# Hybrid decoder step: block choice, sample softmax and attention in one stage of two interleaved threads

## The chip, the cores and the metric

One core of one Trainium2 chip. The metric is device time in microseconds (us) of one execution of the whole kernel; less is better. TensorE is also called PE, VectorE DVE, ScalarE ACT, GpSimd POOL; SP is the queue that mostly issues DMAs.

## The reference

One inference step of a two-layer decoder, all in float32, on a prompt of 512 tokens and on 8 sample sequences of 4 new tokens each, whose past of 4096 tokens lies in a paged cache (32 pages of 128 tokens a sequence, found by a page table). A layer applies one input projection, four parallel mixers (convolution, pooling, sparse attention, gated DeltaNet), an output projection and a feed-forward. The change concerns the sparse attention, with 4 heads, 2 key/value heads (two heads share one) of 64 channels. Each query is answered by three branches, whose outputs are weighted by gates and added:

```python
kc = compress_blocks(k_cmp, ...)            # branch 0: one key per 16 tokens
p_cmp = masked_softmax(q . kc + bias, d_cmp >= 0)
imp = p_cmp summed over the 64-token blocks
top = the 16 best blocks (first, current and previous forced)
o_sel = softmax over the tokens of those blocks . v_sel    # branch 1
o_win = softmax over the last 512 tokens . v_win           # branch 2
o = g0 * o_cmp + g1 * o_sel + g2 * o_win
```

The scores get a relative position bias. For the prompt, 512 tokens are 8 blocks, so all are selected and branch 1 is causal attention.

## The kernel before

Activations are kept transposed (channels on partitions): S.xT is the residual stream, S.yT collects the mixers' outputs, S.HT the projection. A loop runs over the two layers. Inside it, each `stage` (L151) is a block in which every engine has its own instruction stream, tied to the others by semaphores; a stage ends with a barrier of all engines (L161). A layer's stages in order: projection, convolution and pooling, natural_keys, sample_scores (L884), then the part of this change, then gated_delta (L1511, first stage "gnorm") and mix_and_feed_forward.

sample_scores loads keys and values to be compressed and keys to be scored, compresses keys and values of the cache, and leaves the raw scores of the samples: rows are the 128 (sequence, head, token) triples, columns are tokens, in p_sel (128 x 4128) and p_win (128 x 544). At L989 and L1033 it uses weights of 32 columns whose results go to four groups of 32 PSUM partitions.

The part of this change consists of three stages in before:

- **"top"** (sample_softmax, L1156). Gates, softmax of branch 0 over 255 compressed keys, sums per block, and two rounds of "eight largest" give block_bias (L1226), which is a large negative number for blocks that are not selected. PE also computes the compressed values (L1184). Nearly all of it is a chain on DVE with short trips to PE and ACT.
- **"soft"** (L1230). DVE adds block_bias to p_sel (L1254) and takes the maximum (L1264), ACT computes the exponential (L1281). PE then multiplies each 128-column piece with a diagonal of gate over sum (L1244), which transposes and scales it at once; ten groups of tiles are copied to st_sel, st_win and pt_new.
- **"att"** (attention_outputs, L1292). The prompt's work is cut into N = 48 units (query tile i, head h, branch br). A unit: scores on PE (L1383, contraction of 64 rows), bias and maximum on DVE (L1482 to L1484), exponential on ACT (L1451), transpose on PE (L1393), copy on ACT (L1461), values on PE (L1407), and the product with the gate over the sum on DVE, added to o (L1499, L1502); the widths are 31 or 128 (i + 1) columns. PE's stream runs three units at once, one step apart. Between them stands sample_third (L1353): for sequence b and half h of its pages, a third of the 16 matmuls of L1373, whose weights are 16 columns of st_sel and whose moving data is one page of cached values, 128 x 128. All 40 matmuls of a sequence go into one 16-row accumulation. A float32 matmul is carried out as two instructions, a transpose as one.

The cached values come as DMAs of one page each, 128 rows of 512 bytes (L1330), 256 pages per layer. Two buffers of 16 pages (vsel) hold one half of a sequence each. SP issues 12 of the 16 pages of a half and ACT, between its own work, 4. The page number must be in a register of the issuing queue, which page_numbers (L554) loads four at a time (L557). SP also loads the window values (L1340), 256 KB, and at the start the bias strip (L1346):

```python
for h in range(2):
    if not first:
        sp.wait_ge(s.part, b * 2 + (h - 1))
    ...
    for first_page in range(0, by_sp, 4):
        fetch(sp, mybir.EngineType.SP, b, h, first_page, pages[h])
```

s.part counts halves that PE has summed. An engine's instructions are issued in the order written; a wait holds up all that stands behind it on that engine.

## Time and profile before

| | us |
|---|---|
| median of 3 runs | 3021.0 (3011.27 to 3021.8) |
| the profiled execution, its own time | 3015.42 |
| its span, first to last instruction | 3013.5 |
| PE busy | 2706.2 |
| DVE busy | 916.5 |
| ACT busy | 578.1 |
| POOL busy | 237.3 |
| "top", "soft" and "att" in the first layer | 528.65 to 737.3 |
| the same in the second layer | 2014.0 to 2218.8 |

Times of the rows count from the span's start. In a list by line, a row gives line, engine, operation, output <- inputs, shape, count, then busy time in us, mean ns of one, and the idle time of the engine before them with what ended it. PEld is the weight load, which runs beside PE. A row of a stretch gives its ends and length, then busy time and, in brackets, instructions of PE, PEld, DVE, ACT and POOL, as far as they are asked for, then the granted clock of TensorE (1.00 is 2.4 GHz, 0.50 is 1.2 GHz), the DMA engines' busy share and GB/s. SPq and ACTq are the queues' DMA instructions.

### The profile page before, as it was taken

What the parts mean: (1) busy time and instruction counts of PE and PEld (TensorE: products, weight loads), DVE (VectorE), ACT (ScalarE), POOL (GpSimd) and SP (SyncE); (2) the same over time, 40 slices, a digit from 0 to 9 for tenths busy, and PEclk for the clock granted to TensorE, in tenths of its full rate; (3) what the DMA queues carried; (4) which work ended last, traced back from release to release, by engine and by line L of the source; (5) the groups of instructions that cost most, each with busy time, mean ns of one, the idle gap of its engine ahead of it and who ended that gap; (6) DMA issues with size and microseconds to landing.
All of it is one profiled execution on the core that took longest, in us unless ns stands there. A gap on an engine that the chain in (4) does not pass through costs nothing. (4 is left out here: it accounts for less than half of the span.)

```text
span 3013.5 us, 45104 instructions
## 1 busy us (share of the span) xinstructions
PE 2706.2 (90%) x17236; PEld 2206.2 (73%) x17236; DVE 916.5 (30%) x2207; ACT 578.1 (19%) x1224; POOL 237.3 (8%) x328
## 2 busy tenths in 40 slices
PE   6996999698698999999969879978968989999997
PEld 4885887566585888888758668865757768888885
DVE  2742333443543210000118223343544322110002
ACT  0013332223310200000110223322242103000002
POOL 0500000000130100000005000000002101000000
PEclk8997999789695999999979989997987779999998
DMA  5205775242001134022042257733410021331220
GB/s 193 78 28 157 223 222 157 82 118 79 2 22 50 48 106 126 28 66 74 0 139 70 49 188 220 219 98 111 126 43 1 22 92 42 111 113 28 56 56 30
DMA packets 343596, 276.93 MB, mean 92 GB/s; under 512 B 61473, under 2 KB 339106, under 8 KB 343002
## 3 DMA queue, kind: packets, MB, share of 16 engines
q1 hardware_dynamic: 316840, 253.71, 28.6%
q10 hardware_dynamic: 26546, 20.35, 2.2%
q8 instruction: 140, 2.29, 0.3%
q14 instruction: 70, 0.57, 0.1%
HBM read 264.14 MB, written 18.17 MB: 94 GB/s over the span
## 5 line engine op out<-in xcount | busy, mean ns | idle before, releaser
L2169 PE MATMUL psum<-xT,up_ring 128*128 128x272 f32 x2048 | 470.3, 392 | 0.0
L2169 PEld LDWEIGHTS psum<-xT,up_ring 128*128 128x128 f32 x2048 | 389.1, 190 | 80.3
L2188 PE MATMUL psum<-ff,HT 128*128 128x272 f32 x1536 | 353.6, 392 | 0.0
L2188 PEld LDWEIGHTS psum<-ff,HT 128*128 128x128 f32 x1536 | 291.8, 190 | 60.2
L368 PE MATMUL psum<-xT,w_ring 128*128 128x272 f32 x1408 | 326.9, 395 | 7.8 <-PEq L161 4.0
L368 PEld LDWEIGHTS psum<-xT,w_ring 128*128 128x128 f32 x1408 | 269.3, 192 | 65.2 <-DMA w_ring<-in_w_in 4.7
L979 PE MATMUL psum<-cst,cache 128*128 128x128 f32 x1600 | 208.9, 286 | 17.8 <-DMA cache<-in_cache_nsa_kv 11.6
L979 PEld LDWEIGHTS psum<-cst,cache 128*128 128x128 f32 x1600 | 179.0, 145 | 40.4 <-DMA cache<-in_cache_nsa_kv 13.0
L2032 DVE SCALAR_TENSOR_TENSOR xT<-xT,psum 128x544 f32<-128x544 f32 (+1 forms) x42 | 24.2, 584 | 527.9 <-PE psum L2188 441.6
L1009 PEld LDWEIGHTS psum<-chunks,W 64*128 64x128 f32 x2304 | 132.8, 189 | 16.8 <-ACT st_sel L1089 11.7
L1373 PE MATMUL psum<-vsel,st_sel 128*16 128x128 f32 x1024 | 136.4, 286 | 9.2 <-DMA vsel<-in_cache_nsa_kv 9.2
L1009 PE MATMUL psum<-chunks,W 64*128 64x128 f32 (+1 forms) x2304 | 139.5, 277 | 0.0
L2234 DVE TENSOR_SCALAR ff<-psum 128x544 f32<-128x544 f32 x32 | 23.2, 724 | 378.7 <-PE psum L2169 378.7
L1373 PEld LDWEIGHTS psum<-vsel,st_sel 128*16 128x16 f32 x1024 | 97.2, 101 | 47.1 <-issue 17.6
L1009 PEld LDWEIGHTS psum<-st_sel,W 64*128 64x128 f32 x2048 | 116.8, 188 | 16.1 <-ACT chunks L1089 11.7
L2146 PE MATMUL psum<-yT,HT 128*128 128x272 f32 x512 | 121.8, 400 | 5.2 <-PEq L161 5.2
L2286 ACT ACTIVATE ln_sq<-xT 128x272 f32<-128x272 f32 x64 | 22.4, 426 | 531.1 <-DVE xT L2201 531.1
L1009 PE MATMUL psum<-st_sel,W 64*128 64x128 f32 x2048 | 122.9, 275 | 0.0
L2146 PEld LDWEIGHTS psum<-yT,HT 128*128 128x128 f32 x512 | 98.9, 194 | 26.2 <-issue 5.5
L2188 PE MATMUL psum<-ff,yT 128*128 128x272 f32 x512 | 118.0, 392 | 0.0
L1820 POOL TENSOR_TENSOR lm<-lt,cst 128x512 f32<-128x512 f32 (+1 forms) x50 | 63.7, 1277 | 647.2 <-SPq L159 572.0
L2188 PEld LDWEIGHTS psum<-ff,yT 128*128 128x128 f32 x512 | 97.3, 190 | 20.1
(423 smaller groups left out, 3160.4 us busy)
## 6 DMA issues: line engine op xcount, KB each, us to landing
cache<-in_cache_nsa_kv SPq DMA_DIRECT2D x512, 192.0 KB, 2.8
up_ring<-in_w_up SPq DMA_DIRECT2D x32, 1024.0 KB, 5.1
vsel<-in_cache_nsa_kv SPq DMA_DIRECT2D x384, 64.0 KB, 1.9
HT<-in_w_down SPq DMA_DIRECT2D x12, 2048.0 KB, 9.0
w_ring<-in_w_in SPq DMA_DIRECT2D x20, 1024.0 KB, 5.1
vsel<-in_cache_nsa_kv ACTq DMA_DIRECT2D x128, 64.0 KB, 2.2
HT<-in_w_out SPq DMA_DIRECT2D x8, 1024.0 KB, 5.9
yT<-in_w_down SPq DMA_DIRECT2D x4, 2048.0 KB, 10.3
```

The lines of the kernel that those rows point to most:

```text
L368: last = pe.matmul(psum[0:w.shape[1], 2 * (t % 4) + h, 0:HALF], w, moving(k)[:, h * HALF:(h + 1) * HALF], start=(k == 0), stop=(k == kt - 1))
L979: last = pe.transpose(psum[:, bank, j * P:j * P + P], cache[:, u % slots, j, c * P:c * P + P], C["ident"])
L1009: last = pe.matmul(hidden(q, k, c), W1[r, c, j, :], chunks[q % 2][r, c, j, 0:n], start=(j == 0), stop=(j == 15))
L1373: last = pe.matmul(o, S.st_sel[:, half * h + t, cols], vsel[:, h, t, :], start=False, stop=(h == 1 and t == half - 1))
L1820: pool.tensor_tensor(lm[0:n, m % 2, :, 0:n], DTs(lt, q), bc_mid(C[f"level{v}"][0:n, 0:n], HEADS), ALU.mult).then_inc(s.lm, 1)
L2032: return dve.scalar_tensor_tensor(tile, tile, ALPHA, src, ALU.mult, ALU.add)
L2146: last = pe.matmul(psum[:, 2 * (t % 4) + h, 0:HALF], ring[:, (t // 2) % 3, k, (t % 2) * P:(t % 2) * P + P], yT[:, k, half_of(h)], start=(k ...
L2169: last = pe.matmul(psum[:, 2 * (t % 4) + h, 0:HALF], up_ring[:, g % 3, k, (t % 2) * P:(t % 2) * P + P], xT[:, k, half_of(h)], start=(k == ...
L2188: last = pe.matmul(psum[:, 2 * (t % 4) + h, 0:HALF], down[t % 3][:, k, :], f[:, k, half_of(h)], start=(k == 0), stop=(k == FT - 1))
L2234: dve.tensor_scalar(halves(f[:, t, :]), psum[:, 2 * (t % 4):2 * (t % 4) + 2, 0:HALF], 0.0, None, ALU.max).then_inc(s.u_rect_dve, 1)
L2286: act.activation(sq[:, k, :], xT[:, k, half_of(h)], ACT.Square).then_inc(s.squared, 1)
```

## The change

The three stages become one, "att" (function attention), with one barrier. Each engine but SP and POOL has two threads, sample() and prompt(), written as generators and merged in a fixed order: four steps of the sample thread, then one prompt step and one sample step in turn. The sample thread's steps: 0 to 3 are "top", 4 to 8 the additions to p_sel, its maximum and exponential, 9 to 18 the ten transposed tiles (p), 19 to 26 one whole sequence each (b), 27 the end.

- The sample sums: the matmuls of a sequence are dealt to four accumulations in four groups of 32 PSUM partitions (weights of 32 columns, of which the other 16 belong to the neighbouring sequence); a product with a new constant, "fold", picks and adds the four parts at the end.
- The prompt units: N = 24, each with two heads of different key/value heads. The gate over the sum is multiplied into the exponentials by GpSimd (normed), and PE adds the three branches in PSUM with the transposed result, so that neither o nor its transposes remain.
- The page buffers: four instead of two. Two are the weights W1, which are no longer needed; two lie in p_sel, and SP and ACT wait for the last transposed tile (s.pt_turned) before they load into them. SP issues 10 pages of a half, ACT 6, and page numbers are loaded two at a time. The loop on SP is written out.
- ACT issues its 6 pages of both first halves as its first instructions; the later ones stand at the end of step 18 and in the steps of the sequences.

```diff
-                    sample_softmax(S, l, c)
-                attention_outputs(S, l, cmp)
+                    attention(S, l, c)
...
+def in_turn(order, **threads):
+
+
+    for name in order:
+        next(threads[name], None)
+    for t in threads.values():
+        for _ in t:
+            pass
+
+
+def attention_order(n_top, n_units, n_values):
+
+
+    order = ["t"] * 4
+    for k in range(n_units):
+        order += ["c"]
+        if k < n_top - 4:
+            order += ["t"]
+    return order
...
+    half = NPG // 2
+    vsel = [S.W1[:, c, :, :] for c in range(2)]
+    vsel += [p_sel[:, 2048 * c:2048 * c + 2048].rearrange("p (j n) -> p j n", n=P) for c in range(2)]
+    pt = S.hid[:, 0, :, :].rearrange("p b n -> p (b n)").rearrange("p (s k n) -> p s k n", s=2, k=KVH)
+    o_s = S.hid[:, 1, 0:4, :].rearrange("p b n -> p (b n)").rearrange("p (b n) -> p b n", b=NB)
+    NQ = NPG // 4
+    NG = NQ + 2
+    n_top = 9 + NG + NB + 1
+    order = attention_order(n_top, N + 4, NB)
+    by_sp = 10
...
+        def fetch(eng, kind, hh, first, n, loaded):
+            for j in range(first, first + n, 2):
+                for i, page in enumerate(page_numbers(S, kind, hh // 2, half * (hh % 2) + j, 2)):
+                    src = layer(io.cache_nsa_kv, l)[ds(page, 1)].rearrange("a t c k d -> (a t) (c k d)")
+                    eng.dma_start(vsel[hh % 4][:, j + i, :], src[:, 3 * P:4 * P]).then_inc(loaded, 16)
+
+        @block.sync
+        def _(sp):
+            src = bass.AP(io.line_dram.tensor, 127, [[LINE - 1, P], [P * LINE, HEADS], [1, STRIP]])
+            sp.dma_start(strip[:, :, :], src).then_inc(s.strip, 16)
+            for hh in range(2 * NB):
+                b = hh // 2
+                if hh in (2, 3):
+                    sp.wait_ge(s.pt_turned, NG)
+                if hh >= 4:
+                    sp.wait_ge(s.part, hh - 3)
+                if hh % 2 == 0:
+                    if b:
+                        sp.wait_ge(s.part, 2 * b - 1)
+                    src = layer(io.cache_win_kv, l)[b].rearrange("(j p) c k d -> p j c (k d)", p=P)
+                    sp.dma_start(vwin[:, :, :], src[:, :, 1, :]).then_inc(s.window, 16)
+                fetch(sp, mybir.EngineType.SP, hh, 0, by_sp, pages[hh % 4])
...
+                for p in range(NG):
+                    if p == 0:
+                        pe.wait_ge(s.new_added, 5)
+                        pe.wait_ge(s.diag, 3)
+                    if p == 1:
+                        pe.wait_ge(s.ptc_copied, 1)
+                    if p == 2:
+                        pe.wait_ge(s.vc_copied, 4)
...
+                for b in range(NB):
+                    cols = slice(32 * (b // 2), 32 * (b // 2) + 32)
+                    o = [psum[32 * c:32 * c + 32, b % 3, 0:P] for c in range(4)]
+                    if b == 0:
+                        pe.wait_ge(s.pt_act, NG // 2)
+                        pe.wait_ge(s.pt_dve, NG // 2)
+                    if b >= 3:
+                        pe.wait_ge(s.s_dve if (b - 3) % 2 else s.s_act, (b - 3) // 2 + 1)
+                    pe.matmul(o[0], pt_new[:, 0, cols], S.kv_s[:, 3 * P:4 * P], start=True, stop=False)
+                    pe.matmul(o[1], pt_new[:, 1, cols], S.kv_s[:, 5 * P:6 * P], start=True, stop=False)
+                    for j in range(2):
+                        pe.matmul(o[2 + j], pt_cmp[:, j, cols], S.vc[:, j, b, :], start=True, stop=False)
+                    pe.wait_ge(s.window, 16 * b + 16)
+                    for j in range(4):
+                        pe.matmul(o[j], pt_win[:, j, cols], vwin[:, j, :], start=False, stop=False)
+                    for h in range(2):
+                        hh = 2 * b + h
+                        pe.wait_ge(pages[hh % 4], 16 * by_sp * (hh // 4 + 1))
+                        pe.wait_ge(more[hh % 4], 16 * (half - by_sp) * (hh // 4 + 1))
+                        for t in range(half):
+                            last = pe.matmul(o[t % 4], pt_sel[:, half * h + t, cols], vsel[hh % 4][:, t, :], start=False,
+                                             stop=(h == 1 and t >= half - 4))
+                        last.then_inc(s.part, 1)
+                    yield
...
+            def turn(n):
+                pe.wait_ge(s.normed, n + 1)
+                if n:
+                    pe.wait_ge(s.pt_copied, n)
+                w = width(n)
+                for k in range(KVH):
+                    for j in range(0, w, P):
+                        m = min(P, w - j)
+                        last = pe.transpose(psum[0:m, 5 + k, j:j + P], sc[:, n % 3, k, j:j + m], C["ident"])
+                last.then_inc(s.turned, 1)
...
+                for n in range(N + 3):
+                    if n < N:
+                        scores(n)
+                    if 2 <= n < N + 2:
+                        turn(n - 2)
+                    if n >= 3:
+                        values(n - 3)
+                    yield
...
+            def fetch_rest(hh):
+                fetch(act, mybir.EngineType.Activation, hh, by_sp, half - by_sp, more[hh % 4])
...
+                fetch_rest(0)
+                fetch_rest(1)
+                yield
+                act.wait_ge(s.maxed, 1)
+                act.activation(pc[:, 4:4 + NCB], pc[:, 4:4 + NCB], ACT.Exp, bias=stat[:, 0, 0:1], accum_out=stat[:, 0, 1:2]).then_inc(s.exped, 1)
...
+                    if p == NG - 1:
+                        act.wait_ge(s.pt_turned, NG)
+                        fetch_rest(2)
+                        fetch_rest(3)
+                    yield
...
+                for b in range(NB):
+                    if 2 * b + 4 < 2 * NB:
+                        act.wait_ge(s.part, 2 * b + 1)
+                        fetch_rest(2 * b + 4)
+                        act.wait_ge(s.part, 2 * b + 2)
+                        fetch_rest(2 * b + 5)
+                    if b % 2 == 0:
+                        act.wait_ge(s.part, 2 * b + 2)
+                        act.wait_ge(s.vc, 4)
+                        act.copy(o_s[:, b, :], psum[:, b % 3, 0:P]).then_inc(s.s_act, 1)
+                    yield
...
+            def normed(n):
+                w = width(n)
+                pool.wait_ge(s.coef, n + 1)
+                for k in range(KVH):
+                    x = sc[:, n % 3, k, 0:w]
+                    last = pool.tensor_scalar(x, x, coef[:, n, k:k + 1], None, ALU.mult)
+                last.then_inc(s.normed, 1)
+
+            for n in range(N):
+                normed(n)
...
+                dve.tensor_tensor(x, psum[:, 3:5, 0:w], bias, ALU.add).then_inc(s.biased, 1)
+                dve.wait_ge(s.biased, n + 1)
```

## Rows read from the trace of the kernel before

**Rows 1.** The page of the profile, engine totals of the whole span.

```profile
PE 2706.2 (90%) x17236; PEld 2206.2 (73%) x17236; DVE 916.5 (30%) x2207; ACT 578.1 (19%) x1224; POOL 237.3 (8%) x328
```

**Rows 2.** Busy time by stretch: removed stages, then attention stage; sum of both layers.

```profile
528.65:562.50 33.85, 16.44 (x120) 15.76 (x120) 19.47 (x39) 11.84 (x17) 0.00 (x0) 0.75 0.00 1
562.50:737.30 174.80, 159.23 (x1040) 113.63 (x1040) 77.09 (x340) 44.08 (x154) 0.00 (x0) 0.89 0.42 120
...
sum 413.45, PE 347.76 PEld 257.04 DVE 193.22 ACT 111.91 POOL 0.00; mean PE 86.94 PEld 64.26 DVE 48.31 ACT 27.98 POOL 0.00
```

**Rows 3.** Timeline of the SP queue, first layer: start us, us, what, xcount.

```profile
650.33 0.39 SPq L1340 DMA_DIRECT2D vwin<-in_cache_win_kv  x1
651.39 16.87 SPq L1330 DMA_DIRECT2D vsel<-in_cache_nsa_kv  x24
668.98 0.39 SPq L1340 DMA_DIRECT2D vwin<-in_cache_win_kv  x1
```

**Rows 4.** Waits of the SP queue, attention stage, first layer: us in total, times, longest.

```profile
SPq L1340 <- PE psum L1373: 13.6, 4, 6.2
```

**Rows 5.** Lines L1330 and L557: issues and page-number loads, ns min/median/max.

```profile
L1330 SPq DMA_DIRECT2D vsel<-in_cache_nsa_kv x384: 332/333/1473, 564.2 to 2208.7; - x192
...
L1330 ACTq DMA_DIRECT2D vsel<-in_cache_nsa_kv x128: 339/340/1651, 563.5 to 2208.3; - x128
...
L557 SPq TENSOR_LOAD <-pages x224: 293/298/506, 265.1 to 2206.2; - x112
```

**Rows 6.** Groups of PE from 676 to 720 us.

```profile
L1373 PE MATMUL psum<-vsel,st_sel 128*16 128x128 f32 x140 | 17.5, 273 | 0.0
```

**Rows 7.** Line L1033, 256 columns in four strips: ns of one; its stretch, busy us (count).

```profile
L1033 PE MATMUL psum<-cache,q_pad x16: 379/379/379, 526.5 to 2012.7; 128*32 128x256 f32 x16
...
526.48:527.72 1.24, 1.23 (x16) 0.51 (x15) 1.00 0.00 0
```

**Rows 8.** DMA rate in 40 slices of the attention stage, first layer.

```profile
GB/s 159 363 277 105 64 0 167 128 111 128 131 150 33 76 101 67 135 144 93 142 130 158 96 126 127 164 95 81 143 129 158 79 136 58 154 138 83 147 10 0
```

**Rows 9.** Timeline of ACT, 524 to 571 us.

```profile
528.61 1.28 ACT L1195 ACT_TABLE_LOAD   x1 [3.44 <-PEq L161]
...
545.72 3.73 ACT L1281 ACTIVATE p_sel<-p_sel,stat 128x4128 f32<-128x4128 f32 x1 [11.87 <-DVE stat L1264]
...
563.46 5.41 ACTq L1330 DMA_DIRECT2D vsel<-in_cache_nsa_kv  x8
```

**Rows 10.** Timeline of DVE, 524 to 571 us.

```profile
530.86 0.16 DVE L1214 RECIPROCAL stat<-stat 128x1 f32<-128x1 f32 x1 [0.67 <-ACT pc L1195]
...
534.65 0.26 DVE L1227 TENSOR_SCALAR block_bias<-block_bias,sbias 128x65 f32<-128x65 f32 x1
535.71 4.42 DVE L1254 TENSOR_TENSOR p_sel<-p_sel,block_bias 128x4096 f32<-128x4096 f32 x1 [0.80 <-PEq L161]
...
541.23 4.45 DVE L1264 TENSOR_REDUCE stat<-p_sel 128x1 f32<-128x4128 f32 x1
```

**Rows 11.** Timeline of PE, 518 to 570 us.

```profile
550.32 9.60 PE L1244 MATMUL psum<-diag,p_sel 128*128 128x128 f32 x64 [14.01 <-DVE diag L1270]
```

**Rows 12.** Busy time and granted clock by stretch, first layer.

```profile
550.00:555.00 5.00, 4.68 (x22) 4.68 (x23) 1.56 (x5) 0.87 (x3) 0.00 (x0) 0.51 0.01 3
...
606.20:626.60 20.40, 19.88 (x81) 12.59 (x81) 4.54 (x21) 2.63 (x10) 0.00 (x0) 0.50 0.34 97
```

**Rows 13.** Lines L665 and L667: multiplications on GpSimd, ns min/median/max.

```profile
L665 POOL TENSOR_SCALAR pd<-sum,cst x8: 1963/1998/2710, 128.8 to 1625.4; 64x496 f32<-64x496 f32 x8
...
L667 POOL TENSOR_SCALAR pd<-sums,cst x8: 904/994/1645, 131.6 to 1628.2; 64x32 f32<-64x32 f32 x8
```

**Rows 14.** Groups of the prompt units, attention stage, first layer.

```profile
L1451 ACT ACTIVATE sc<-sc,nmax 128x512 f32<-128x512 f32 x8 | 5.8, 722 | 19.5 <-DVE nmax L1484 19.5
...
L1482 DVE TENSOR_TENSOR sc<-psum,strip 128x512 f32<-128x512 f32 x8 | 5.5, 692 | 5.7 <-PE psum L1383 5.7
...
L1461 ACT COPY pt<-psum 128x512 f32<-128x512 f32 x8 | 4.6, 571 | 2.4 <-PE psum L1393 2.4
```

More of the change, by code:

```diff
@@ L1511, in gated_delta, with prompt @@
+            def prompt():
+                for n in range(N + 3):
+                    if n < N:
+                        biased(n)
+                    if 1 <= n <= N:
+                        coefficient(n - 1)
+                    if n >= 3 and (n - 3) % 3 == 2:
+                        out(n - 3)
+                    yield
+            in_turn(order, t=sample(), c=prompt())
 def gated_delta(S, l, ctx):
```

545 lines of the change are left out of this document (245 added, 300 removed).

## The prediction

> **What bounds the kernel now.** I read the page first: PE is busy for 90% of the span [rows 1], which points to TensorE as the thing to relieve. Then the busy time by stretch [rows 2]: the part that the change rewrites is 33.85 us (the two stages "top" and "soft") and 174.80 us (stage "att") in the first layer, 413.45 us in both. In "top" and "soft" PE works for half the time and nothing moves by DMA; in "att" PE is busy for 159 of 175 us. Only the third view, the SP queue's timeline, shows a second bound in "att". One sequence's 24 page loads are issued in 16.87 us, and with the window load and the first page numbers ahead of them that is 17.9 of the 18.65 us from one sequence to the next (650.33 to 668.98) [rows 3]. SP waits for TensorE for 13.6 us in the whole stage, in four pieces [rows 4]. A page of 64 KB costs its queue a 333 ns issue (340 on ACT) and, every four pages, a 298 ns register load of page numbers [rows 5]; with address arithmetic and the rare long issue (up to 1473 ns) [rows 5] the 24 pages of [rows 3] come to about 0.61 us a page and 0.35 us a load. So "att" has two limits of nearly one height, TensorE and the issuing of small DMAs. The change lowers the first by much and the second by little.
>
> **The change, part by part** (times from the first instruction of the merged stage, at 528.65 us in before).
>
> Sample sums in strips. A sequence has 40 matmuls, each two instructions, 80 in all. Now they follow one another: 140 take 17.5 us, 0.125 us each at the full clock [rows 6]. Four 32-column strips side by side: 16 instructions of 256 columns take 1.24 us; less the 379 ns of the last one, that is 0.86 us for 15, 0.057 us each [rows 7]; with 128 columns I take half, 0.029 us, with 0.125 us as the other end. A sequence falls from 10 to 2.3 us of TensorE, 62 us per layer. That is off the path if the pages come at SP's pace, which is the next point.
>
> Page loads. SP now issues 10 pages of a half instead of 12, ACT 6, but page numbers are loaded two at a time. On SP a half costs 10 x 0.61 + 5 x 0.35 = 7.85 us. Two halves have free buffers (W1) from the start; the other two buffers lie in p_sel, free only when the last of ten transposed tiles is done, and SP's wait for that holds up everything behind it. The remaining 14 halves and 7 windows (0.6 us each) are 14 x 7.85 + 4 = 114 us of issuing after that moment; ends 106 (0.58 and 0.30 us, no long issue) and 124 (0.65 and 0.42 us). In addition SP, before the second window's load, waits for the first half's sums, one prompt step later: 4 us (3 to 6). ACT has 6 pages and three loads a half, 4.4 us, 8.8 a sequence, beside a prompt step of 2.8 us, which fits into SP's 16.3 us. In the two busiest slices the DMA engines moved 363 and 277 GB/s [rows 8]; at their mean, 320, a page takes 0.2 us of transfer against 0.61 us of issue, and the 16.5 MB of the 14 halves and 7 windows take 52 us against 114. The Trainium skill, "DMA: Bandwidth & Descriptors", section "Issuing engines are not separate DMA queues", says that issuing from several engines at once only saves the sequencer's time, "which is usually small relative to the DMA itself". For these pages the rows say the opposite; by that rule the term would be 52 us.
>
> The serial front. It must be done before SP can go on. ACT first issues its share of both free halves: 8 pages took 5.41 us [rows 9], so 12 pages with six loads take 8.7 us, then the 1.28 us table load [rows 9], then the first exponential: done at 10.9 us, where DVE could go on 2.2 us after the first instruction before [rows 10]. From there to block_bias 3.8 us as now (530.86 to 534.91) [rows 10]: 14.8 us. Then DVE alternates the 4.42 us addition in two halves, the 4.45 us maximum [rows 10] and prompt units of 1 to 1.5 us: maximum done at 27.7 us; ACT's unit, then the 3.92 us exponential over p_sel (3.73 us and its sum) [rows 9], to 34.2 us, three small DVE operations, 35 us (33 to 38). In before the same work ended 21.6 us in (550.3) [rows 11].
>
> Ten steps "tile and prompt unit" follow. DVE needs 2.1 to 2.4 us for one, GpSimd about 2.9: its multiplication by a per-partition scalar takes 994 ns for 32 elements and 1998 for 496 [rows 13], so 1.45 us for 256 elements, two a unit, less for the short branch. TensorE needs 0.9 us for a tile and 1.0 for a unit at the full clock (64 instructions in 9.60 us, half of them at the low clock [rows 11]) and 3.75 us at 1.2 GHz. After an idle stretch it starts low: 550 to 555 us had 0.51 while fully busy, and from 606 to 627 us it stayed at 0.50, busy throughout [rows 12]. I take nearly three steps at 3.75 and the rest at 2.9: 30 us (22 with DVE's pace; 42 with GpSimd's long cases, 2710 ns [rows 13]). The last tile is done at 65 us.
>
> The tail. The last half lands 2 us after its issue and is summed in 0.8 us. Only then are the last unit's scores computed, and its chain is exposed: scores 0.9 (four times the four instructions of 256 columns of [rows 7], at 0.057), bias and maximum 2.7 (two heads, 0.69 us each and operation [rows 14]), two exponentials 1.65 [rows 14], coefficient 0.55 (three operations of 0.16 us [rows 10] and their waits), GpSimd 4.1 (two at 2.0 [rows 13]), transposes 1.0 and values 1.0 (eight times 0.125 each [rows 6]), copy 1.1 [rows 14], out and semaphores 1.1: 14.1 us, 15 with part of it at 1.2 GHz. Together 18 us (14 to 22).
>
> The remaining edits (pairs of heads, no output transposes, one stage end instead of three) shorten work on all engines and are inside these terms; what hides them is SP's issuing. If that cover is gone, TensorE's own 2.3 us of sums and 2.6 us of a prompt unit are what shows per sequence.
>
> **Sum:** 35 + 30 + 4 + 114 + 18 = 201 us per layer, 402 in both against 413.5: 11.5 us less. An idle TensorE leaves the next stage at 1.2 GHz; I add 1 us per layer, an estimate between nothing and 3. The net is -9.5 us on the profiled execution's own 3015.4 us; that execution lies 5.6 us under the median of the three runs, 3021.0, within their spread, so I forecast 3011 us for the median.
>
> **Rivals.** (1) The issue rate is no bound, and the loads go at the data rate worked out above: 52 us for 114, 62 less per layer, 2887 us. For it: the strips make TensorE quick. Against it: SP's packed rows [rows 3] and its few waits [rows 4]. Chance 0.05. (2) The strips do not run side by side, so the change does not do what it says: 10 us of sums and 2.6 of prompt in each 16.3 us, still hidden at 2.4 GHz, but 25 us at 1.2 GHz until the clock rises; some 10 us per layer, 3030 us. Against it: [rows 7]. Chance 0.08, half of it within 0.5%. (3) Slower: the front takes GpSimd's pace. The place is the ten steps with SP waiting behind them; at 4.4 us a step they take 42 us, the tail 3 us more, with issuing at 116 us: 35 + 42 + 4 + 116 + 21 = 218 us, 3045 us. It decides for slower once a layer's stage exceeds 213 us, that is 12 us over my sum. Against it: the median of the GpSimd rows. Chance 0.15. (The Trainium skill, "GPSIMD Engine Reference", section "Engine selection", calls a one-input operation there roughly line-rate; the 1998 ns for 496 elements [rows 13], where DVE needs 0.69 us for 512 [rows 14], disagree.) (4) Front and tail quick: steps of 2.3 us, issuing 110 us, tail 14 us: 35 + 22 + 3 + 110 + 14 = 184 us, 2972 us. Chance 0.12.
>
> **How the numbers follow.** The forecast has 0.60: 0.20 of it faster by over 0.5% (15 us, about what a measurement of this kernel can tell from no change), 0.37 within, 0.03 slower. Faster: 0.20 + 0.05 + 0.12 = 0.37. Within: 0.37 + 0.04 = 0.41. Slower: 0.03 + 0.04 + 0.15 = 0.22. All low ends together give 178 us a layer, 2960 us; all high ends 232 us and over 3065, which needs every term at its worst. The range goes from 2957 to 3045 us, with rival 1 and the worst of 3 left out.
>
> **What the profile would show.** Right: SP packed with issues from the tenth tile to the last page at 7.8 us a half, TensorE waiting for vsel there at a clock near 0.5, strip instructions 0.03 us apart, ACT's first exponential 10 us after the stage's start. Wrong: the stage ends before 185 or after 213 us; SP's issues below 0.5 us a page; or SP waiting for TensorE while the sums run.

## The result and the profile after

The changed kernel takes 3055.9 us (median of 4 runs, 3053.51 to 3068.86) against 3018.3 us before (4 runs, 3011.27 to 3021.8): a ratio of 1.0136, 95% interval 1.0101 to 1.0172. It is slower by 37.6 us, and 11 us beyond the top of the forecast range. The profiled execution is the longest of the four (3068.9 us, span 3067.0); in it the merged stage lasts 226.4 us in the first layer from its first TensorE instruction to its last work, and the next stage's first TensorE instruction comes at 227.7 and 227.1 us in the two layers. The same distance before was 209.3 and 205.4 us. The two stages thus lost 18.4 and 21.7 us, 40 in all, about as much as the medians differ (37.6). The two profiled executions differ by 53.5 us in span; the other 13 us lie outside the two stages. Over all traces of this document that rest takes between 2595 and 2617 us, so what an edit does is read from the stages rather than from a median alone.

The page's engine totals, against [rows 1]:

```profile
PE 2623.6 (86%) x17236; PEld 2133.1 (70%) x17236; DVE 851.2 (28%) x1805; ACT 567.2 (18%) x1180; POOL 325.4 (11%) x424
```

TensorE works 83 us less and the kernel is slower: the busiest engine was relieved, and the time went elsewhere. Of GpSimd's 88 us more, 84 are the new normalisation.

Busy time by stretch of the merged stage in the first layer, against [rows 2]. The cuts are where the prediction has its terms: the last `diag`, the last tile, SP's first issue behind its waits, its last page, the end. Columns: stretch, length, busy us (count) of PE, PEld, DVE, ACT and POOL, granted clock, DMA share, GB/s.

```profile
529.83:565.90 36.07, 17.56 (x82) 13.69 (x82) 21.45 (x60) 13.29 (x35) 5.82 (x8) 0.56 0.40 118
565.90:600.70 34.80, 30.28 (x198) 20.81 (x198) 19.01 (x57) 15.81 (x56) 11.90 (x18) 0.82 0.00 1
600.70:609.10 8.40, 6.01 (x78) 4.63 (x82) 1.82 (x8) 1.45 (x6) 4.92 (x4) 0.60 0.23 64
609.10:735.45 126.35, 55.43 (x690) 35.62 (x682) 16.37 (x40) 15.52 (x46) 13.36 (x14) 0.64 0.45 127
735.45:756.20 20.75, 16.02 (x122) 11.95 (x122) 5.30 (x15) 4.21 (x9) 6.20 (x4) 0.59 0.03 7
```

The fourth stretch is the one to look at: 126 of 226 us, in which no engine is busy for half the time, and the DMA engines work for 0.45 of it. The timeline of the SP queue in it, against [rows 3]:

```profile
609.07 0.39 SPq L1249 DMA_DIRECT2D vwin<-in_cache_win_kv  x1
610.22 16.00 SPq L1233 DMA_DIRECT2D p_sel<-in_cache_nsa_kv  x20
626.46 0.38 SPq L1249 DMA_DIRECT2D vwin<-in_cache_win_kv  x1
```

From one window load to the next are 17.39 us for 20 pages (17.4 to 18.9 in the whole stage, 18.1 in the mean); before it was 18.65 us for 24, of which SP's own work was 17.9. ACT took over a sixth of SP's pages and SP's time a sequence did not fall. Why stands in the register loads of page numbers (ns min/median/max), against [rows 5]:

```profile
L557 SPq TENSOR_LOAD <-pages x288: 293/472/507, 264.4 to 2242.0; - x144
L557 ACTq TENSOR_LOAD <-pages x96: 484/495/687, 529.8 to 2215.0; - x96
```

SP's 288 loads include 128 of four numbers in an earlier stage. The 70 behind the release in the first layer, all of two numbers, take 467/474/492 ns; the 48 loads of four in before's "att" took 296/302/314. SP now makes five loads a half, 2.37 us, where it made three, 0.91 us. That is 1.5 us more, and the two page issues that it saved are worth 1.2 us: nine of the sequence's ten loads lie inside the row of 20 pages, so a page is (16.00 - 9 x 0.474) / 20 = 0.59 us. Before its first window behind the release, SP sat for 60.8 us in one wait, having nothing it was allowed to issue:

```profile
SPq L1247 <- PE psum L1318: 60.8, 1, 60.8
```

And TensorE's waits in the fourth stretch are for those pages:

```profile
PE psum L1318 <- DMA p_sel<-in_cache_nsa_kv: 32.5, 7, 6.9
PE psum L1318 <- DMA W<-in_cache_nsa_kv: 30.6, 6, 7.7
```

### The profile page after: what moved, and what is told of

The parts are those of the page before. It is cut to its first block and busy times, and to the rows that moved or that the text cites. A ratio compares the mean times of both kernels' runs of the same rounds, so it can differ in the third digit from the quotient of the medians.

```text
span 3067.0 us, 44341 instructions
## 1 busy us (share of the span) xinstructions
PE 2623.6 (86%) x17236; PEld 2133.1 (70%) x17236; DVE 851.2 (28%) x1805; ACT 567.2 (18%) x1180; POOL 325.4 (11%) x424
## 5 line engine op out<-in xcount | busy, mean ns | idle before, releaser
L979 PE MATMUL psum<-cst,cache 128*128 128x128 f32 x1600 | 212.4, 289 | 17.4 <-DMA cache<-in_cache_nsa_kv 11.2
L979 PEld LDWEIGHTS psum<-cst,cache 128*128 128x128 f32 x1600 | 182.5, 147 | 40.1 <-DMA cache<-in_cache_nsa_kv 12.7
L1009 PEld LDWEIGHTS psum<-chunks,W 64*128 64x128 f32 x2304 | 133.1, 190 | 17.1 <-ACT st_sel L1089 11.7
L1468 POOL TENSOR_SCALAR sc<-sc,coef 128x31 f32<-128x31 f32 (+4 forms) x96 | 84.4, 893 | 374.7 <-DVE coef L1579 374.3
L1318 PE MATMUL psum<-p_sel,st_sel 128*32 128x128 f32 x512 | 29.3, 402 | 79.0 <-DMA p_sel<-in_cache_nsa_kv 79.0
L2395 ACT ACTIVATE pos<-psum 128x544 f32<-128x544 f32 x32 | 20.0, 624 | 395.0 <-PE psum L2257 395.0
```

The lines of the kernel that those rows point to most:

```text
L979: last = pe.transpose(psum[:, bank, j * P:j * P + P], cache[:, u % slots, j, c * P:c * P + P], C["ident"])
L1009: last = pe.matmul(hidden(q, k, c), W1[r, c, j, :], chunks[q % 2][r, c, j, 0:n], start=(j == 0), stop=(j == 15))
L1318: last = pe.matmul(o[t % 4], pt_sel[:, half * h + t, cols], vsel[hh % 4][:, t, :], start=False, stop=(h == 1 and t >= half - 4))
L1468: last = pool.tensor_scalar(x, x, coef[:, n, k:k + 1], None, ALU.mult)
L2395: act.activation(halves(pos[:, :]), psum[:, 2 * (t % 4):2 * (t % 4) + 2, 0:HALF], ACT.Relu).then_inc(s.u_rect_act, 1)
```

## Experiments

Every run is the changed kernel with one edit, unless it says otherwise. "Next stage" is the time from the stage's first TensorE instruction to the next stage's first, in layers one and two; it is 227.7 and 227.1 us in the changed kernel, its last tile 70.8 and 70.7, its last page from SP 205.3 and 204.6. The kernel before was timed beside each batch (medians 3020.7, 3018.8 and 3022.2 us). The theories: (1) SP's issuing of pages, in series behind the release of `p_sel`, sets the pace; (2) GpSimd's normalisation does; (3) the low TensorE clock does; (4) the strips bring the gain that the change hoped for.

**e3: fewer pages by SP, page numbers by four.**

```
-    by_sp = 10
+    by_sp = 8
-            for j in range(first, first + n, 2):
-                for i, page in enumerate(page_numbers(..., half * (hh % 2) + j, 2)):
+            for j in range(first, first + n, 4):
+                for i, page in enumerate(page_numbers(..., half * (hh % 2) + j, 4)):
```

> The changed kernel, with 8 of the 16 pages of a half on each queue and page numbers loaded four at a time instead of two. In the changed kernel SP needs 16.5 us for the 20 pages of a sequence and 17.7 from one sequence to the next, a register load of two numbers taking 0.48 us. If the issuing of pages sets the pace (theory 1), SP's part of a half falls to 8 x 0.58 + 2 loads, some 5.4 us, and the two queues' shares are nearly equal: a sequence then takes 12 to 14.5 us, bound by ACT, which also has the exponentials; the stage is 22 to 38 us shorter per layer and the kernel 45 to 75 us shorter than the changed one, about 2985 to 3010. If the multiplications on GpSimd (theory 2) or the low clock of TensorE (theory 3) set the pace between the tenth tile and the end, the stage stays within 5 us. The front, up to the tenth tile, is the same under all, less 1 to 2 us.

Measured: 2969.5 us (4 runs, 2966.31 to 2972.38), ratio to before 0.9835 (0.9805 to 0.9864): faster than both kernels, and below the expected 2985 to 3010, since a sequence took 11.7 us and was not held to 12 to 14.5 by ACT. Next stage at 184.3 and 184.8 us. The timeline of its SP queue:

```profile
604.97 0.39 SPq L1249 DMA_DIRECT2D vwin<-in_cache_win_kv  x1
605.94 10.49 SPq L1233 DMA_DIRECT2D p_sel<-in_cache_nsa_kv  x16
616.67 0.38 SPq L1249 DMA_DIRECT2D vwin<-in_cache_win_kv  x1
```

its register loads:

```profile
L557 SPq TENSOR_LOAD <-pages x192: 293/298/503, 264.3 to 2146.6; - x192
```

and two stretches, the ten steps and SP's issuing:

```profile
561.82:596.62 34.80, 30.29 (x198) 20.86 (x200) 19.03 (x57) 15.81 (x56) 11.85 (x18) 0.82 0.00 1
...
605.98:688.21 82.23, 54.97 (x666) 35.89 (x666) 16.38 (x40) 15.50 (x46) 13.32 (x14) 0.67 0.68 191
```

What follows: the steps last 34.80 us to the digit as in the changed kernel, GpSimd and TensorE are as busy in them, and the granted clock is as low (0.67 against 0.64 while pages are issued). Only SP's part shrank: from its first window load behind the release to its last page it was 126.4 us and is 83.5 (604.97 to 688.50; the row above begins with the first page), 43 less, and the time fell by 86 us, twice 43. Theory 1 is shown for the main part. Theory 3 falls for this stretch: the clock stayed and the time went. The data rate rose to 191 GB/s, so it had not been the bound either.

**e8: the split alone.** As e3 but with the page numbers still by two (`by_sp = 8` is its only edit), to tell which half of e3 brings what.

> The changed kernel with SP issuing 8 pages of a half and ACT 8, page numbers still loaded two at a time (the split alone; e3 also loaded four at a time). Theory 1 (SP's sequencer is the bound after the release of p_sel, and a load of two costs 0.47 us where a load of four costs 0.30): a half costs SP four pairs at 1.65 us = 6.6 us, 14 halves and 7 windows 100 us, so the last page is issued some 18 us later than in e3 (163 us into the stage) and 25 us earlier than in the changed kernel (205 us): 181 us; time about 3005 us. A rival in which the gain of e3 is the split alone and the size of a load does not matter: last page at 163 us, 2969 us.

Measured: 3021.0 us (one run); SP's last page at 183.3 and 182.2 us, forecast 181; next stage at 204.5 and 203.6 us. The time is 16 us above the expected 3005, although the last page came nearly as forecast: in this execution the rest of the kernel took 2611 us, in e3's 2595. Its SP queue:

```profile
613.06 0.39 SPq L1249 DMA_DIRECT2D vwin<-in_cache_win_kv  x1
614.20 12.64 SPq L1233 DMA_DIRECT2D p_sel<-in_cache_nsa_kv  x16
627.08 0.38 SPq L1249 DMA_DIRECT2D vwin<-in_cache_win_kv  x1
```

A sequence's 16 pages take 14.0 us here and 11.7 in e3 (the window load's distance). The issuing lasts 99.7 us against 82.2, 17.5 us for 56 loads of two in place of 28 of four; by the medians, 56 x 0.467 less 28 x 0.298, it is 17.8. So of e3's 43 us a layer the size of the load brings 18 to 20, by the issuing and by the next stage's start, and the split the rest. In this split the loads by two cost about as much a layer as the change lost.

**e2: more pages by SP, loads of four.** `by_sp = 12`, the split of the kernel before.

> The changed kernel, with the old split of 12 pages on SP and 4 on ACT and page numbers loaded four at a time. It tells SP's issuing from ACT's: SP has 12 x 0.58 + 3 loads a half, 8.0 us if a load of four numbers takes 0.30 us as in the kernel before, 8.3 if it takes 0.48 as in the changed one; ACT has 2.7 us a half instead of 4.9. Theory 1 with SP as the bound: the part from the tenth tile to the last page stays within 4 us of 126 us per layer, the front is 3 us shorter because ACT issues 8 instead of 12 pages ahead of its first exponential. If ACT's share were what delays the sequences, that part would fall by 20 us or more.

Measured: 3042.5 us (one run); next stage at 219.0 and 216.3 us, SP's part 121.5 us where it was 126.4. With two more pages a half for SP it is still quicker than 10 pages with loads of two, and with a third fewer pages for ACT it gains only 5 us: ACT's share did not set the pace.

**b1: the same split in the kernel before.** Was the kernel before held up by SP too?

```
-        by_sp = 12
+        by_sp = 8
-                fetch(act, ..., by_sp, pages_act[part % 2])
+                for first in range(by_sp, half, 4):
+                    fetch(act, ..., first, pages_act[part % 2])
```

> The kernel before the change, with SP issuing 8 of the 16 pages of a half and ACT 8 instead of 12 and 4, page numbers four at a time as in that kernel. It tells whether the kernel before was bound by TensorE or by SP's issuing. If by TensorE (busy 159 of 175 us in that stage): the stage stays within 3 us a layer of the 175 us, 3015 to 3025 us in all, and the gain of e3 needs the strips. If by SP's issuing (my reading of the rows before the prediction, two limits of nearly one height): at most the 13.6 us of SP's waits separate the limits, so the gain is bounded by TensorE's 159 us a layer: 2 to 10 us a layer, 3000 to 3015 us. A gain like e3's (42 us a layer) would mean that the strips were never needed.

Measured: 3075.0 us (4 runs, 3073.49 to 3081.8), ratio 1.0186 (1.0149 to 1.0224): slower, which neither reading expected. SP now waits for TensorE (us in all, times, longest), where it had 13.6 us in four pieces [rows 4]:

```profile
SPq L1340 <- PE psum L1373: 45.9, 7, 14.8
SPq L557 <- PE psum L1373: 38.1, 7, 9.9
```

and ACT's exponentials sit behind ACT's own page issues. The group in this kernel, then in the kernel before (busy, mean | idle before it, and for what), and TensorE's transposes in this kernel, which wait for the exponentials:

```profile
L1452 ACT ACTIVATE sc<-sc,nmax 128x31 f32<-128x31 f32 (+4 forms) x48 | 23.0, 480 | 117.8 <-issue 56.2 <-DVE nmax L1485 46.1 <-PE psum L1373 15.6
```

```profile
L1451 ACT ACTIVATE sc<-sc,nmax 128x31 f32<-128x31 f32 (+4 forms) x48 | 23.1, 481 | 94.4 <-DVE nmax L1484 66.7 <-issue 27.7
```

```profile
L1393 PE MATMUL psum<-cst,sc 128*128 128x128 f32 (+1 forms) x96 | 23.0, 325 | 19.9 <-ACT sc L1452 19.9
```

"issue" is ACT issuing pages: 56.2 us ahead of exponentials instead of 27.7, and TensorE's wait for exponentials grew from 8.3 to 19.9 us. My reading, which no further run tests: one head's unit at a time, 48 units with TensorE waiting for ACT's result within a sequence, has no room for twice the issues. So relieving SP alone made the kernel before slower; in the merged stage the same split with loads of four saves 43 us a layer. Whether the pairs of heads or the strips make that room this run doesn't tell; e9 shows that it is not the strips.

**e5 and e9: the strips undone**, in the changed kernel (e5) and in e3 (e9): all of a sequence's sums go to one group of 32 rows.

```
-                    o = [psum[32 * c:32 * c + 32, b % 3, 0:P] for c in range(4)]
+                    o = [psum[0:32, b % 3, 0:P] for c in range(4)]
```

with the start and stop flags, copies and the fold to match.

> The changed kernel, with all 40 matmuls of a sequence added into one group of 32 PSUM partitions instead of four side by side. If SP's issuing hides the sums (theory 1), TensorE goes from 2.3 to 9 us a sequence at the full clock, 17 at the low one, beside 17.7 us of issuing; it is then busy enough to be given the full clock for most of the time: the kernel stays within 15 us of the changed one, the last sequence's end costs 1 to 3 us per layer. If the sums in strips carry the change's gain (theory 4), undoing them costs 50 us per layer.

> The 8/8 kernel e3 with the strips undone (all sums of a sequence into one group of 32 rows, as in e5), so at an issue pace of 11.7 us a sequence instead of 17.9. Theory 4 (the strips pay only once the issuing is quick; in e5, where SP was the bound, they were worth 7 and 12 us a layer): a sequence then needs 10 us of sums at the full clock and some 3 us for its prompt unit, 13 to 15 us against 11.7 for seven sequences, 10 to 25 us, and the 7 to 12 us of e5: next stage at 200 to 220 us, 3000 to 3040 us. If the strips are worth nothing beyond e5's share: 191 to 196 us, 2985 to 2995 us.

Measured: e5 3090.5 us (one run), next stage at 234.5 and 239.0 us. That is 35 us above the changed kernel, where theory 1 had allowed 15. SP's part is as long as with strips (126.5 and 125.5 us); what grew is the time to SP's first window load behind the release (by 4.1 and 10.0 us, of the latter 4.7 in the tile steps) and the tail (by 2.6 and 2.2): the first half's sums and the last one's are not hidden. e9 3002.1 us (10 runs, 2994.25 to 3010.3), ratio to before 0.9944 (0.9926 to 0.9962), next stage at 194.7 and 194.3 us. A half of e9 on TensorE, and its busy time while SP issues:

```profile
651.23 3.68 PE L1318 MATMUL psum<-p_sel,st_sel 128*32 128x128 f32 x32 [1.39 <-DMA p_sel<-in_cache_nsa_kv]
```

```profile
612.45:699.25 86.80, 77.57 (x668) 66.61 (x666) 16.34 (x40) 14.06 (x41) 13.32 (x14) 0.98 0.63 178
```

Two halves with strips, in the changed kernel:

```profile
637.65 1.93 PE L1318 MATMUL psum<-W,st_sel 128*32 128x128 f32 x32 [3.26 <-DMA W<-in_cache_nsa_kv]
...
728.22 1.08 PE L1318 MATMUL psum<-p_sel,st_sel 128*32 128x128 f32 x32 [1.06 <-DMA p_sel<-in_cache_nsa_kv]
```

32 instructions take 3.68 us in a row, at a granted clock of 1.00 during them. In strips 32 take 1.93 us at a granted clock of 0.50, as in twelve of the last fourteen halves (1.91 to 1.94 us, clock 0.50 to 0.52), and 1.08 us at 1.00. So the strips do run side by side, and the second rival falls. At the same clock they are 3.4 times as quick: 0.034 us an instruction, near the 0.029 that the prediction took for the full clock [rows 7]. At the low clock, where the changed kernel mostly runs them, an instruction takes 0.060 us, and the gain over e9's row at the full clock is a factor of 1.9. They are worth 7 and 12 us a layer in e5 and 10 in e9, so in the changed kernel, where SP was the bound, they brought no more than that. e9's stage came in below its expected 200 to 220 us and inside the 191 to 196 of the alternative, that the strips are worth nothing beyond e5's share; its time is inside the first range. TensorE was busy for 77.6 of 86.8 us and nearly kept up: SP waited for its sums for 5.8 us in four pieces beside the long wait, and its part took 88.1 us for e3's 83.5. Even without strips the merged stage with the better split beats the kernel before by half a per cent.

**e6: the normalisation on DVE.** The GpSimd block is dropped and its two multiplications follow the coefficient on DVE.

> The changed kernel with the prompt heads' normalisation on DVE instead of GpSimd and nothing else. Theory 2 (the third rival of the prediction: GpSimd's pace sets the ten steps): the steps from the diagonal (36 us) to the last tile (70.8) shrink from 34.8 to 25 us, SP's wait for the first half from 8.4 to about 4, the tail from 20.8 to 17: 18 us a layer, 3020 us, which would make GpSimd the whole of the loss against the kernel before. Theory 1 (SP's issuing, 125 us a layer, is the main part, and GpSimd only some microseconds ahead of it and behind it): steps 30 us, tail 17 to 18, last page 6 to 8 us earlier, next stage at 217 to 219 us: 3037 to 3041 us.

Measured: 3052.2 us (4 runs, 3040.39 to 3055.9), ratio 1.0102 (1.0073 to 1.0131). Its interval and the changed kernel's overlap, and theory 1's 3037 to 3041 us was missed as well. In its trace the ten steps take 31.6 and 32.5 us (34.8), the next stage comes at 216.9 and 220.3 us: 10.8 and 6.9 less, and the span is 12.9 us shorter than the changed kernel's; the medians differ by 3.7 us only, because the changed kernel's profiled execution lies 13 us above its median and this one 3.7. So the stage gained what theory 1 expected of it (217 to 219 us), and the time did not show it. Theory 2 expected 18 us a layer. What GpSimd costs in the changed kernel is in these rows, its widest and narrowest multiplications and TensorE's waits in the ten steps:

```profile
L1468 POOL TENSOR_SCALAR sc<-sc,coef 128x512 f32<-128x512 f32 x8 | 12.4, 1567 | 46.8 <-DVE coef L1579 46.8
...
L1468 POOL TENSOR_SCALAR sc<-sc,coef 128x31 f32<-128x31 f32 x16 | 7.8, 504 | 88.2 <-DVE coef L1579 88.2
```

```profile
PE psum L1347 <- ACT hid L1442: 4.0, 4, 2.5
PE psum L1347 <- POOL sc L1468: 2.7, 2, 1.5
```

TensorE waits for GpSimd for 2.7 of the 34.8 us and for ACT for 4.0. It is itself busy for 30.3. So the pace of the ten steps was mostly TensorE's, and the third rival, which had them at GpSimd's, falls as the main cause. Its sign was right, and its share is not nothing: the 7 to 11 us a layer that e6 gains, against 25 us a layer by which the forecast was missed.

**e1: ACT's first issues later.** Its 12 pages go behind the copy of the turned compressed probabilities instead of ahead of the first exponential.

```
             def sample():
-                fetch_rest(0)
-                fetch_rest(1)
                 yield
...
                 act.copy(pt_cmp[:, :, :], ...).then_inc(s.ptc_copied, 1)
+                fetch_rest(0)
+                fetch_rest(1)
                 yield
```

> The changed kernel with ACT's first 12 page issues (9.5 us) moved from ahead of its first exponential to behind the copy of the turned compressed probabilities. Theory 1 (everything up to the release of p_sel is in series with SP's issuing): the front to the diagonal shortens by up to 8.8 us (DVE's wait of 8.9 us), diag at about 27.5 instead of 36 us, tiles at 62, last page at 197, 8 us less a layer, 3040 us. If instead the exponential over p_sel is delayed by the same issues further on, or the ten steps stretch, diag stays above 33 us and the time within 5 us of the changed kernel's.

Measured: 3055.9 us (4 runs, 3054.93 to 3060.32), ratio 1.0127 (1.0089 to 1.0165): no change against the changed kernel (next stage at 227.6 and 222.5 us). In the changed kernel ACT and DVE read

```profile
531.04 9.48 ACTq L1233 DMA_DIRECT2D W<-in_cache_nsa_kv  x12
540.55 1.28 ACT L1390 ACT_TABLE_LOAD   x1 [14.20 <-issue]
```

```profile
542.48 0.16 DVE L1497 RECIPROCAL stat<-stat 128x1 f32<-128x1 f32 x1 [8.92 <-ACT pc L1390]
```

and in this one

```profile
534.67 0.51 ACT L1388 ACTIVATE pc<-pc,stat 128x255 f32<-128x255 f32 x1 [0.90 <-DVE stat L1485]
...
540.18 9.30 ACTq L1233 DMA_DIRECT2D W<-in_cache_nsa_kv  x12
549.53 0.32 ACT L1435 ACTIVATE sc<-sc,nmax 128x31 f32<-128x31 f32 x1 [9.94 <-issue]
```

```profile
550.28 0.17 DVE L1577 TENSOR_SCALAR coef<-esum 128x2 f32<-128x2 f32 x1 [6.51 <-ACT sc L1435]
```

The first exponential comes 2.2 us into the stage, but the issues now stand ahead of the first prompt exponential, and DVE, which goes through sample and prompt in one written order, waits 6.5 us for that instead of 8.9 us. The diagonal comes at 34.3 us instead of 36.0, but the last tile at 73.9 and 68.5 us instead of 70.8 and 70.7. Moved within one chain, the work mostly renamed the wait.

**e4: two halves released earlier.** SP waits for 4 and 8 tiles instead of 10 ahead of halves 2 and 3, and issues the second window behind both.

```
-                    sp.wait_ge(s.pt_turned, NG)
+                    sp.wait_ge(s.pt_turned, 4 * hh - 4)
```

> The changed kernel, with SP allowed into each half of p_sel as soon as the four tiles that read it are transposed (4 and 8 of 10) instead of after all ten, and with the first of those loads ahead of the second window's. Theory 1: SP issues the two halves, 16.5 us, inside the front, where it is idle for 61 us, so 12 halves instead of 14 remain after it: the stage is 15 to 18 us shorter per layer, the kernel 30 to 36 us shorter than the changed one. Theories 2 and 3: nothing changes, since GpSimd and TensorE do the same work in the same order.

Measured: 3039.8 us (4 runs, 3032.05 to 3047.09), ratio 1.0073 (1.0047 to 1.0098); the last page and the next stage come 11 us earlier, not 15 to 18. The rest stands in SP's waits for sums, the window of a sequence (L1254) and the half behind it (L1252):

```profile
SPq L1254 <- PE psum L1324: 7.8, 1, 7.8
SPq L1252 <- PE psum L1324: 6.8, 1, 6.8
```

The single window buffer takes its turn in SP's order: the third window waits for the second sequence's sums, and the pages behind it wait with it.

**e7: e3, e1, e4 and e6 together.**

> The changed kernel with all the cures together: 8/8 split with loads of four, the parts of p_sel released at tiles 4 and 8 instead of 10 (e4), ACT's first issues later (e1), and the normalisation on DVE instead of GpSimd. Theory 1: each shortens the chain front, release, SP's issuing, tail. From e3 (diag 36, tiles 72, last page 163, next stage 184 us): front 8 less, release 8 to 10 earlier, tail 3 less (three quarters of the 6.2 us of GpSimd in the last unit), DVE more in the steps by 0.5 us each (5 more): next stage at 167 to 172 us, 2969 less twice 12 to 17: 2935 to 2945 us. If with 8/8 ACT or the DMA engines set the pace, the last page stays at 163 us or above and the time at 2960 us or more.

Measured: 2956.9 us (4 runs, 2954.76 to 2971.13), ratio 0.9811 (0.9767 to 0.9855), next stage at 171.6 and 175.9 us, 12.8 and 8.9 us less than in e3; 12 to 17 were expected, and 2935 to 2945 us. The same stall, now in the open:

```profile
572.07 16.22 SPq L1233 DMA_DIRECT2D p_sel<-in_cache_nsa_kv  x16
593.64 13.58 SPq L1254 DMA_DIRECT2D vwin<-in_cache_win_kv  x2
607.81 10.10 SPq L1233 DMA_DIRECT2D W<-in_cache_nsa_kv  x16
```

SP is done with both halves of `p_sel` at 588.3 and issues the next pages at 607.8: 19.5 us for two window loads, which the second row holds together, each behind a wait for sums.

**e10: built from the runs.** Split and loads as in e3, normalisation on DVE, release at 4 and 8 tiles. SP, idle in the front, issues all 16 pages of halves 0 and 1, ACT none. A window is loaded just ahead of the first pages that wait for later sums than it does.

```
+            window(0)
             for hh in range(2 * NB):
                 if hh in (2, 3):
-                    sp.wait_ge(s.pt_turned, NG)
+                    sp.wait_ge(s.pt_turned, 4 * hh - 4)
                 if hh >= 4:
                     sp.wait_ge(s.part, hh - 3)
+                if hh >= 4 and hh % 2 == 0:
+                    window(hh // 2 - 1)
+                fetch(sp, ..., hh, 0, half if hh < 2 else by_sp, pages[hh % 4])
+            window(NB - 1)
```

> A version built from what the runs so far show: 8/8 split with loads of four; SP, idle for 61 us in the front, issues all 32 pages of the first two halves, ACT none of them; the parts of p_sel released at tiles 4 and 8; each window loaded only after the pages that could go ahead of it (in e7 SP sat from 588 to 607 us behind two window loads); normalisation on DVE. Theory 1: front to the diagonal 26 to 28 us (36 less ACT's 9.5), last tile at 56, issuing of 14 halves and 7 windows 82 us of which some 10 lie beside the tiles, tail 18: next stage at 147 to 157 us against 171.6 and 175.9 in e7: 2915 to 2930 us. If the tile steps and the prompt units with DVE's load set the pace instead (24 to 26 steps of 3 us and more after the diagonal are some 110 us with the sums), it ends at 160 to 165 us: 2935 to 2945 us. Sure to be wrong if above e3's 2969 us.

Measured: 2928.9 us (5 runs, 2924.35 to 2935.33), ratio to before 0.9702 (0.9682 to 0.9723), 127 us less than the changed kernel. The diagonal comes at 27.9 us in both layers, the last tile at 61.0 and 56.9, the next stage at 163.7 and 160.4. Its SP queue:

```profile
533.74 22.00 SPq L1233 DMA_DIRECT2D W<-in_cache_nsa_kv  x32
575.91 16.45 SPq L1233 DMA_DIRECT2D p_sel<-in_cache_nsa_kv  x16
600.24 0.39 SPq L1243 DMA_DIRECT2D vwin<-in_cache_win_kv  x1
601.21 11.61 SPq L1233 DMA_DIRECT2D W<-in_cache_nsa_kv  x16
```

and two stretches, the ten steps and SP's issuing behind them:

```profile
560.22:593.25 33.03, 30.62 (x198) 21.00 (x198) 23.46 (x75) 15.67 (x56) 0.00 (x0) 0.79 0.11 31
...
601.23:672.29 71.06, 45.94 (x600) 33.26 (x596) 18.04 (x47) 11.22 (x35) 0.00 (x0) 0.69 0.72 201
```

The total is inside theory 1's range at its edge; the stage is not at 147 to 157 us but where the alternative put it. The ten steps still take 33 us with TensorE busy for 30.6 of them, without GpSimd and with less waiting: their pace is mostly TensorE's work at a granted clock of 0.79. The 32 free pages are issued in 22 us inside SP's former wait, and ACT is free for its exponentials. How much of the 28 us that e10 gains on e7 is theirs and how much the windows' was not separated.

## Why the prediction was wrong

The frame held. The chain front, ten steps, SP's wait, issuing, tail was the right one, SP was packed through it, TensorE waited for pages at a low clock, and the view that had to be read was the SP queue's. All five terms came out larger than forecast, two of them, the wait and the issuing, above their upper ends. First layer (in the changed kernel the second ends 0.6 us earlier; in e10 SP's issues for halves 2 and 3 lie beside the tiles, 12 halves stand behind the wait, and the column runs to the next stage's first instruction, 1.3 us after the last work):

| term | forecast | measured | in e10 |
|---|---|---|---|
| front to the diagonal | 35 (33 to 38) | 36.1 | 27.9 |
| ten steps | 30 (22 to 42) | 34.8 | 33.0 |
| SP's wait for the first half | 4 (3 to 6) | 8.4 | 7.0 |
| issuing of 14 halves, 7 windows | 114 (106 to 124) | 126.4 | 72.4 |
| tail | 18 (14 to 22) | 20.8 | 23.4 |
| sum | 201 | 226.4 | 163.7 |

- **The step that failed** is "On SP a half costs 10 x 0.61 + 5 x 0.35 = 7.85 us". The 0.35 us a load comes from loads of four numbers [rows 5], the only ones this line had before. I took a load of two to cost no more than a load of four. It costs 474 ns by its median against 302. Less 4.2 us for the seven windows, a half measured (126.4 - 4.2) / 14 = 8.73 us. At 0.474 instead of 0.35 us the 70 loads behind the release are 8.7 of the 12.4 us by which the term was missed. The rest is the page: (8.73 - 5 x 0.474) / 10 = 0.636 us for 0.61, long issues included. The same sum gives 0.63 us a page in e3 (loads at 0.30) and in e8 (loads at 0.474), so one page price fits all three, and only the load's differs. e8 and e3 isolate it: 17.5 us a layer between the two sizes. The rows before gave no price for a load of two, and even the upper end, 0.42 us, lay below what one costs.
- **How much hangs on it.** The issuing makes 12.4 of the 25.4 us by which a layer was missed. With that term as forecast, my estimate is 226.4 - 12.4 = 214 us a layer against before's 208.7 and 204.8: some 14 us slower in all, inside the forecast range and still of the wrong sign. The other half is the ten steps (4.8), the wait (4.4), the tail (2.8) and the front (1.1).
- **A page on that price.** The Trainium skill, "DMA: Bandwidth & Descriptors", section "Latency and other measured facts", gives a register load a floor of about 600 ns and says that the compiler unrolls it four times "to amortize". By the rows a load of four takes 302 ns and one of two 474, so the floor does not hold here. What unrolling would bring no run here tests.
- **Ten steps.** I had 0.9 us for a tile and 1.0 for a unit on TensorE at the full clock, and let GpSimd's 2.9 us set most of them. Measured, GpSimd is below my forecast (3.76 us for four multiplications of 256 elements, 0.94 each, for 1.45; 1.57 for 512, for 2.0), yet a step takes 3.48 us, because TensorE's 198 instructions are busy for 30.3 us at a clock of 0.82, 3.0 a step. The prices from two other tiles [rows 13] were too high, and TensorE's own work, 0.9 + 1.0 us a step at the full clock, was too low: in the last two fifths of the steps, at a granted clock of 1.00, it is still busy for 11.3 of 13.7 us. That the first steps run at the low clock was right (0.50 in the first 7.1 us).
- **SP's wait.** It holds not "one prompt step" but a unit of 384 elements on GpSimd, then the first half's sums:

```profile
600.87 4.92 POOL L1468 TENSOR_SCALAR sc<-sc,coef 128x384 f32<-128x384 f32 x4 [2.38 <-DVE coef L1579]
...
606.72 3.25 PE L1318 MATMUL psum<-W,st_sel 128*32 128x128 f32 x62
609.07 0.39 SPq L1249 DMA_DIRECT2D vwin<-in_cache_win_kv  x1
```

- **Tail.** The order of the terms was right (scores, GpSimd, turn, values), but TensorE ran most of it at a granted clock of 0.50: scores 2.08 us for 0.9, the last unit's transposes 1.94 for 1.0. The values took 3.68 us for 1.0, for the clock and because there are 32 instructions where I counted eight. GpSimd had the last two units' multiplications back to back, 6.20 us for 4.1.

```profile
738.80 2.08 PE L1336 MATMUL psum<-HT 64*128 64x512 f32 x4
...
743.97 6.20 POOL L1468 TENSOR_SCALAR sc<-sc,coef 128x512 f32<-128x512 f32 x4 [16.87 <-DVE coef L1579]
...
752.17 3.68 PE L1360 MATMUL psum<-hid,kvn 128*64 128x128 f32 x32
```

- **Small sums.** "Nearly three steps at 3.75 and the rest at 2.9" make 31 us, not 30, and 530.86 to 534.91 is 4.05 us, not 3.8. The 2972 and 2960 us are counted from the profiled execution's 3015.4, the 3011 and 3045 from the median; from the median they would be 2977 and 2965. None of this moves the sign.
- **Right:** ACT's issues ahead of the first exponential (DVE goes on 12.7 us after the start, forecast 10.9; the six loads of two are part of the difference), the diagonal, SP's single long wait, the strips side by side, and that the data rate is no bound. The stated sign of being wrong, a stage that ends after 213 us, came. The rule weighed in the prediction (the Trainium skill, "DMA: Bandwidth & Descriptors", "Issuing engines are not separate DMA queues") would have had the issuing term at 52 us. The runs disagree: 126 us measured, and in e3 two of SP's ten pages of a half given to ACT, with loads of four, took 43 us off it, while the DMA share was 0.45 and became 0.68.
- **Net.** Before, SP was shut out for the 34 us of "top" and "soft" [rows 2] and then worked beside TensorE for nearly all of the 175 us. Now it may issue two halves early, some 17 us of work, but the other fourteen only 79 us into the stage: 45 us later than before, in return for two halves of sixteen. With a sequence's issuing no cheaper than before, 79 + 126 + 21 is more than 34 + 175.

What stays open: why a load of two numbers takes longer than one of four (no run varied it beyond 2 and 4), and whether pairs of heads or the one merged order let ACT carry half of the issues. Buffers for halves 2 and 3 outside `p_sel`, which would do away with the release, were not tried.

## What to carry to other kernels

When two resources are at nearly the same height, price the change on both, and per item of the queue, not per byte: here two fewer pages a half were bought with two more register loads. Ask of every queue in a new front what it may already do there: SP waited for 61 us while ACT, on the path, issued pages whose buffers were free. And before moving issues onto an engine, look at what is queued behind them: the split of 8 and 8 cost 56 us in the kernel before, and together with loads of four it saved 86 in the changed one.

## What the runs showed of the hardware

- A register load of two page numbers took 474 ns on SP and 495 on ACT (medians, changed kernel's merged stage); of four, 300 and 311 (e3's).
- Four 32-column strips beside each other gave 32 instructions of 128 columns in 1.08 us at a granted clock of 1.00 and 1.93 us at 0.50, against 3.68 us in a row at 1.00. In the changed kernel's stretch TensorE was busy for 55 of 126 us at a mean clock of 0.64, in e9's for 78 of 87 at 0.98.
- GpSimd's multiplication by a per-partition scalar took 0.50 us for 128 x 31 elements and 1.57 us for 128 x 512; on DVE, in e6, 0.24 and 0.48 us.
